# Two-layer backbone on one core: the next layer's norm woven into the layer end, gate blocks moved into the router, the attention's weight pairs reordered

## The reference

```python
shift1, scale1, gate1, shift2, scale2, gate2 = split(silu(c) @ w_mod[l] + b_mod[l], 6)
h = rms_norm(x, norm1_w) * (1 + scale1) + shift1
u_a, v_a, q, k, v, f_in, g = split(h @ w_in)         # 1024 -> 7680
y_a = chunk_gmlp(u_a, v_a, ...)                      # spatial gating, chunks of 128
y_b = diff_attention(rope(norm(q)), rope(norm(k)), v, lam)   # 8 heads, two maps each
y_c = fourier_mix(f_in)
merged = sum over b of sigmoid(g_b) * (y_b @ w_br_b)
x = x + gate1 * (merged @ w_out)
h2 = rms_norm(x, norm2_w) * (1 + scale2) + shift2
# router: 1 of 4 groups, then the top 2 of its 4 experts; 16 experts, D_EXPERT = 512
y = sum over e of gates[:, e] * ((silu(h2 @ w_g[e]) * (h2 @ w_u[e])) @ w_d[e])
x = x + gate2 * y
```

## Time and profile before

| what | value |
|---|---|
| three runs, us | 1627.60, 1633.40, 1635.53 (median 1633.4) |
| profiled execution, us | 1626.59, span 1624.7, granted clock 0.995 |
| PE busy | 1568.7 us, 97% of the span |
| VectorE busy | 1040.4 us, 64% |
| ScalarE busy | 926.4 us, 57% |
| POOL busy | 519.0 us, 32% |
| DMA | 381 MB, 234 GB/s over the span |
| chain that ended last | PE 74%, DMA 11%, VectorE 8%, ScalarE 3% |

### The profile page before, as it was taken

How to read it: one execution, slowest core, us unless ns; L and a number is a source line. 1 busy time by engine, 2 the same in 40 slices (tenths; PEclk the granted TensorE clock), 3 DMA queues, 4 the chain that set the end, 5 groups by cost and what they waited for, 6 DMA issues and landing times.

```text
span 1624.7 us, 21397 instructions
## 1 busy us (share of the span) xinstructions
PE 1568.7 (97%) x7755; PEld 1235.0 (76%) x7755; DVE 1040.4 (64%) x1366; ACT 926.4 (57%) x1298; POOL 519.0 (32%) x263
## 2 busy tenths in 40 slices
PE   7999999999999999999999999999999989999998
PEld 5677877876876787888777778777778768888886
DVE  2226566673354888999962356667633569999997
ACT  4434444444444888888844344544443558888884
POOL 2344554443530311111134446534435221111101
PEclk9999999999999999999999999999999999999999
DMA  9854342334348999999986543422343379999998
GB/s 361 277 202 166 124 131 83 103 122 155 105 168 287 357 383 366 358 370 371 366 253 208 196 165 104 142 91 91 131 145 117 97 270 377 380 381 361 373 381 259
DMA packets 153535, 380.98 MB, mean 234 GB/s; under 512 B 20963, under 2 KB 26789, under 8 KB 153436
## 3 DMA queue, kind: packets, MB, share of 16 engines
q1 hardware_dynamic: 122704, 325.32, 55.9%
q10 hardware_dynamic: 20140, 36.56, 6.4%
q0 software_dynamic: 10592, 17.78, 3.6%
HBM read 377.47 MB, written 27.93 MB: 250 GB/s over the span
## 4 chain that ended last, share of the span: by engine, by line
PE 74%; DMA 11%; DVE 8%; ACT 3%; issue 2%; SPq 0%; POOL 0%; ACTq 0%; DVEq 0%; POOLq 0%
PE ps L611 59%; PE ps L620 5%; DMA raw<-w_e_down 4%; DVE wxl L2521 4%; DMA raw<-w_e_up 3%; PE ps L644 2%; PE ps L961 2%; ACT wxh L1860 1%; DMA raw<-w_mod 1%; DMA y<-part_rows 1%; PE ps L891 1%; PE ps L989 1%; PE ps L1269 1%; PE ps L655 1%; PE ps L663 1%
## 5 line engine op out<-in xcount | busy, mean ns | idle before, releaser
L1999 POOL TENSOR_TENSOR wl<-raw,wh 128x1024 fp32r<-128x1024 f32 x168 | 413.4, 2465 | 521.0 <-ACT wh L1357 505.5
L2521 DVE TENSOR_TENSOR wxl<-raw,wxh 128x1024 fp32r<-128x1024 f32 x384 | 454.3, 1220 | 60.5 <-ACT wxh L1860 58.1
L1860 ACT ACTIVATE wxh<-raw 128x1024 fp32r<-128x1024 f32 x384 | 402.7, 1059 | 92.9 <-DMA raw<-w_e_gate 32.8
L611 PE MATMUL ps<-wxh,xeT 128*128 128x512 f32 x1024 | 342.1, 399 | 5.8 <-DVE xeT L2562 3.3
L1357 ACT ACTIVATE wh<-raw 128x1024 fp32r<-128x1024 f32 x168 | 176.7, 1055 | 220.2 <-PE ps L611 211.7
L611 PE MATMUL ps<-wh,hTh 128*128 128x512 f32 x720 | 294.4, 409 | 3.4 <-DVE hTl L2147 2.6
L611 PE MATMUL ps<-wh,hTl 128*128 128x512 f32 x720 | 282.7, 393 | 0.0
L611 PE MATMUL ps<-wl,hTh 128*128 128x512 f32 x720 | 282.0, 392 | 0.0
L611 PEld LDWEIGHTS ps<-wxh,xeT 128*128 128x128 f32 x1024 | 192.6, 188 | 51.1 <-DVE wxl L2521 5.0
L611 PE MATMUL ps<-wxl,xeT 128*128 128x512 f32 x512 | 199.5, 390 | 0.0
L611 PEld LDWEIGHTS ps<-wh,hTh 128*128 128x128 f32 x720 | 136.1, 189 | 38.7 <-issue 6.8
(11 more groups left out here) (295 smaller groups left out, 2164.4 us busy)
## 6 DMA issues: line engine op xcount, KB each, us to landing
raw<-w_e_gate SPq DMA_DIRECT2D x128, 512.0 KB, 6.8
raw<-w_e_up SPq DMA_DIRECT2D x128, 512.0 KB, 5.7
raw<-w_e_down SPq DMA_DIRECT2D x128, 512.0 KB, 5.6
raw<-w_in SPq DMA_DIRECT2D x120, 512.0 KB, 3.6
own<-w_mod ACTq DMA_DIRECT2D x27, 1024.0 KB, 7.6
raw<-w_mod SPq DMA_DIRECT2D x36, 512.0 KB, 6.0
raw<-w_br_b SPq DMA_DIRECT2D x16, 512.0 KB, 3.7
raw<-w_out SPq DMA_DIRECT2D x16, 512.0 KB, 3.6
```

The source lines that it names most:

```text
L611: ins = pe.matmul(out, act_hl[i], w_hl[j], start=start and n == 0, stop=stop and n == 2)
L1860: act.activation(wxh[:, q % RING_MOE, :, :], raw[:, place, :, :], ACT.Copy).then_inc(sem("hi_done"), 1)
L1999: pool.tensor_tensor(wl[:, p % RING, :, :], raw[:, PAIR_CHUNK[p] % RAW, :, :], wh[:, p % RING, :, :].bitcast(F32), ALU.subtract).then_inc( ...
L2521: dve.tensor_tensor(wxl[:, q % RING_MOE, :, :], raw[:, expert_chunk(l, 0, q)[0], :, :], wxh[:, q % RING_MOE, :, :].bitcast(F32), ALU.subtr ...
```

## The change

It has these parts; the diff names the same functions.

- Attention, both layers: one more pair is pumped ahead of the first head's transposes (`pump(5)`), one less behind them (`pump(1)`). Head 1 loses its extra pair between its scores and `turn_first`, and has one after `turn_second` as the other heads do.
- Layer end, layer 0 to 1. VectorE takes the mean of a tile as soon as its squares are there, and writes only the rows of tile 0 (`front_rows`), between units 3 and 4. For tiles 1 and 2 it computes the reciprocal root alone (`front_rms`) and counts `rms_ready`; ScalarE writes these rows (`front_rows` there). The root of a tile is taken right after its squares.
- ScalarE copies the first of the layer's weight pairs after the squares of tile 1, the second after the rows of tile 2, the third after the first pair of norm columns.
- SP waits for `y` of tile 0 alone before the loads of layer 1.
- Router of the last layer: half (10, 1) takes the place of the filler, half (11, 1) is moved from expert 0 to behind (11, 0).

```diff
--- before.py
+++ after.py
...
             if l:
-                for name in PARTS_IN:
-                    sp.wait_ge(sem(name), at(name, l - 1, PER[name]))
+                sp.wait_ge(sem(PARTS_IN[0]), at(PARTS_IN[0], l - 1, PER[PARTS_IN[0]]))
...
-            pump(4)
+            pump(5)
...
             turn_qk(0)
-            pump(2)
+            pump(1)
             scores(0)
...
                     scores(h + 1)
-                if h == 1:
-                    pump(1)
                 turn_first(h)
                 pump(1)
                 turn_second(h)
-                if h != 1:
-                    pump(1)
+                pump(1)
...
                 part(10, 0)
                 turn_tile(1)
-                spin(FILL_ROUTER[0], 5)
+                part(10, 1)
                 turn_tile(2)
...
                 back(1)
-                part(10, 1)
                 part(11, 0)
+                part(11, 1)
                 back(2)
...
                         token_sums(2, 2, ps[:, 0, 0:2])
-                        if not more:
-                            part(11, 1)
...
+            def front_rows(t):
+
+                act.wait_ge(sem("rms_ready"), t)
+                act.wait_ge(sem("xn_done"), at("xn_done", l, t))
+                act.activation(xn[:, t, :], x[:, t, :], ACT.Copy, scale=st[:, 9 + t:10 + t]).then_inc(sem("xn_done"), 1)
...
-                    if t:
-                        tile_root(t - 1)
-                    hi(DENSE0[l] + t)
-                tile_root(NT - 1)
+                    if t == 1:
+                        hi(DENSE0[l])
+                    if t == NT - 1:
+                        front_rows(1)
+                    tile_root(t)
+                front_rows(2)
+                hi(DENSE0[l] + 1)
...
                 norm_pair(0, R_NORM1, k)
+                if l and k == 0:
+                    hi(DENSE0[l] + 2)
...
+            def front_rms(l, t):
+
+                dve.wait_ge(sem("root"), at("root", l, t + 1))
+                return dve.reciprocal(st[:, 9 + t:10 + t], st[:, 6 + t:7 + t])
+
+            def front_rows(l, t):
+
+                link(front_rms(l, t))
+                dve.tensor_scalar(xn[:, t, :], x[:, t, :], st[:, 9 + t:10 + t], None, ALU.mult).then_inc(sem("xn_done"), 1)
...
-            tile_rows(0)
-            tile_rows(1)
-            tile_rows(2)
+            if l == 0:
+                tile_rows(0)
+                tile_rows(1)
+                tile_rows(2)
...
-            for u in range(NT, 2 * NT):
-                add_unit(u)
-                if l + 1 < DEPTH:
-                    front_mean(l + 1, u - NT)
+            if l + 1 < DEPTH:
+                front_mean(l + 1, 0)
+            add_unit(3)
+            if l + 1 < DEPTH:
+                front_rows(l + 1, 0)
+            add_unit(4)
+            if l + 1 < DEPTH:
+                front_mean(l + 1, 1)
+            add_unit(5)
+            if l + 1 < DEPTH:
+                front_rms(l + 1, 1).then_inc(sem("rms_ready"), 1)
+                front_mean(l + 1, 2)
+                front_rms(l + 1, 2).then_inc(sem("rms_ready"), 1)
```

More of the change, by code:

```diff
@@ L199 @@
     h2_copied=NT, h2_out=16 * (NT + 1), gate_ready=1,
-    pick_ready=PICKED, idx_acc=PICKED, idx_ready=PICKED, table=16 * (2 * NT + 2), pickT_ready=2, scattered0=16 * LOOSE // 2, scattered1=16 * LOOSE // 2, zeroed=16 * 6, parts_in2=16 * 2, parts_added=NT, X_acc=NE + 1, xe_hi=NE + 1, xe_ready=NE + 1,
+    pick_ready=PICKED, idx_acc=PICKED, idx_ready=PICKED, table=16 * (2 * NT + 2), pickT_ready=2, scattered0=16 * LOOSE // 2, scattered1=16 * LOOSE // 2, zeroed=16 * 6, parts_in2=16 * 2, rms_ready=DEPTH, X_acc=NE + 1, xe_hi=NE + 1, xe_ready=NE + 1,
     gathered0=16 * NE // 2 + 16, gathered1=16 * NE // 2 + 32, silu_done=NE,
```

## The result

| | before | changed kernel |
|---|---|---|
| median, us (runs) | 1629.82 (10) | 1619.05 (10) |
| lowest, highest | 1624.88, 1635.53 | 1615.35, 1626.07 |
| profiled execution, span | 1626.59, 1624.7 | 1615.35, 1613.6 |
| granted clock in it | 0.995 | 0.997 |

The ratio is 0.9934 with a 95% interval of 0.9914 to 0.9955: 7 to 14 us, the middle 10.8. The prediction said 1625.6 for the median and 7.75 us. The 57 further runs of the kernel before that were taken beside the experiments have a median of 1628.54, and against them the difference is 9.5 us.

The account below looks back on a forecast made before the run. TensorE, busy 97% of the span, was taken to bound the kernel; 2.8 (attention) + 1.15 (layer end) + 3.8 (gate blocks) = 7.75 us off the 1633.4 median gave 1625.6 us, range 1617.5 to 1632.5.

Parts of the forecast that it names:

- Attention: Both layers: head 1 goes from 14.60 to 13.18 us, 1.4 us gained a layer, 2.8 us in all.
- The moved pair: Ahead of the first head's transposes: pair and transposes change places, the gap of some 1.6 us stays; costed at nothing.
- The layer end, rows and filler: Layer 0 to 1: rows ready about 835.5, PE's filler last at 837.53, so the filler limits the gain.
- the 2.3 us: Layer end: first dense matmul at 840.3 instead of 842.60, before the price of the dead heat.
- The dead heat: Norm: POOL's third subtract beats VectorE's second split by some 0.05 us, PE loses about 1.15; rival R1, VectorE wins, 0.20.
- I take nothing: Layer 1's loads issued earlier: no gain or loss; reads of y have 2.2 us of cover before PE needs them.
- the rule of the round robin: DMA engines alternate between rings: last read of y lands near 825.5 to 827, sum up to 1.5 us smaller.
- gaining 1.15: Layer end: 2.3 us gained less 1.15 us lost to the dead heat; 2.3 kept as the other end.
- ScalarE's issues: Two issues of own<-w_mod ahead of ScalarE's first norm work, 4.21 us before: counted 0, lower end 0.4 us lost.
- The gate blocks: Last layer: half 2.0 and wait for pair 4 2.06 leave expert 0, router loses 0.25; net 3.8 us.
- The wait before expert 1: PE's wait for expert 1's gathered rows: stays at 2.05 us, as VectorE's queue moves with pair 4.
- R2: Rival, chance 0.15: the expert loop returns the head's gain because weights can't follow; all 3.8 us lost, 1629.4 us.

Follow-up runs that it names:

- b3: The changed kernel with SP again waiting for y of all three tiles before the loads of layer 1; one execution, 1619.15 us.
- b2: The changed kernel, filler cut from 30 to 22 rounds, weight copies two and three moved, POOL's third subtract after VectorE's second norm split; median 1614.83 us, ratio 0.992.
- b1: The changed kernel with ScalarE's third weight copy right behind the second instead of behind the first norm pair; ratio 0.9932.
- d1: Against b2: three of the six w_in loads wait for y of all tiles, the other three for tile 0 only; ratio 0.9931.
- a3: The kernel before with the gate-block edits alone, halves (10, 1) and (11, 1) moved in the router; median 1622.43 us, ratio 0.995.

## Why the prediction was right or wrong

**Attention.** Right in its size: 1.40 us a layer, and turn_first doesn't wait in head 1. The moved pair, costed at nothing, costs 0.13 to 0.15 us in layer 1 and about as much in layer 0: the wait is longer by 0.05, and the rest isn't placed. Net 2.5 instead of 2.8.

**The layer end, rows and filler.** Right: the rows were ready 4.3 us after the filler's start (829.49 - 825.15; 5.7 by the forecast's times), the filler was last, and b3 shows the 2.3 us. The row tile on VectorE took 0.75. The cut filler (b2) shows that the rows had room.

**The dead heat.** Right, POOL won by 0.15 us, and the price was 1.1 us as said; b1 takes it away. The Trainium skill (SBUF — State Buffer, "SBUF: two separate sides") names the reason: VectorE with two SBUF inputs and POOL hold a shared port exclusively for a whole instruction. The 2.63 against 0.55 us agrees.

**The loads: the step that failed.** "I take nothing" looked only at the reads of y. Those were covered: the longest took 9.2 us from issue to landing, 8.1 before, and PE didn't wait for it. The 2 to 4 us that the rule of the round robin was weighed with didn't come. Even the 1 us isn't shown to be the loads' doing: over all kernels the longest of the three reads took 8.9 to 10.0 us with six early loads, 8.1 to 8.9 with late ones, and up to 10.4 at the end of layer 1, with no next layer's loads beside it. Nor did the queues take turns at first. In the changed kernel the reads had the DMA engines to themselves from 812.2 to 815.2 us, though five loads were issued by then; its DMA view for that time has one queue:

```profile
q0 software_dynamic: 146, 0.53, 100.2%
```

The first packet of the loads came 2.6 to 4.2 us after their first issue in the eight kernels with early loads, and 1.0 us after it in the four with late ones.

The price came from a place that I hadn't looked at, PE's own pause at the flag, 1.29 us in the earlier trace rows, which I took as fixed. With early loads it is 1.98 to 4.17 us in all eight traces, with late loads 1.29 to 2.11 in four, and half clock followed in five of the eight and in none of the four. Why the pause is longer stays open. The layer end lost 0.5 us in the changed kernel's trace instead of gaining 1.15, which lies within the 0.8 us that unedited layer ends differ by; b3, without that edit, gains 1.11.

**ScalarE's issues.** Hidden, as said: 0.96 us where they took 4.21.

**The gate blocks.** The half and the wait for pair 4 went, 4.06 less the 0.32 that VectorE still costs. The wait before expert 1, which I left at 2.05, fell to 1.27, and the router lost 0.36 instead of 0.25. Net 4.2 instead of 3.8; R2 is wrong, the loop gives nothing back.

**The sum.** 2.5 - 0.5 + 4.2 = 6.2 us from the parts against 7.75. The timed 9.5 to 10.8 us contain something more. The mean granted clock of the timed runs is 0.9954 against 0.9939, which is 2.4 us at 1.71 for each 0.00106 (one stretch in some 1620 us). With it the parts come to 8.6, inside the interval of 7.3 to 14; the -0.5 already holds 0.9 us of half clock on the filler, so the two overlap by up to that. So the forecast was near for two reasons that partly cancel: a price that it missed, and a gain in clock that it didn't know of, and of which only a part has a place. That the size came out so near is partly luck. The median itself came 6.5 us under the 1625.6 of the forecast: 3.6 of these are the level, since the three runs that it started from had a median of 1633.4 and the ten have 1629.82. (The range's lower end is a slip of 0.2: 1626.6 less 8.9 is 1617.7.)

## What to carry to other kernels

Before a load is moved ahead, list every wait near it that DMA engines may have a part in, a pause at a branch among them, and not only the transfers that the diff names. A wait that the view calls "issue" isn't a constant; look at it in several traces. Where the work behind a filler is shortened, shorten the filler with it: here that, with the copies set apart, took 4.65 us off a layer end that the edits alone had left as it was, and 3.1 in d1, where half clock fell on the filler.

## What the runs showed of the hardware

A half-clock stretch had one size, some 3.4 us at 0.50 of the full clock with 1.71 us lost (one was twice that). Leaving out the one at the end of each trace, two to seven of them stood in each profiled execution. They stand behind places where PE had been idle, for 0.8 to 4.2 us, but not behind each of them, and filling the likeliest place moved them to the next in three cases of four. In the changed kernel's ten runs, from 1615 to 1626 us at clocks from 0.997 to 0.992, time and clock go closely together (correlation -0.89). Over the runs of all kernels, each taken against its own mean, they do so less (-0.66), and in a3's twelve runs not at all, so the clock is a part of the spread and not shown to be most of it.

TensorE's pause at a flag's read took 1.29 to 4.17 us and ended 1.42 to 1.46 us behind a packet of an instruction queue, while VectorE's at the same flag stayed at 1.52 to 1.54. Loads issued while POOL's accumulating reads were under way sent their first packet 2.6 to 4.2 us after the issue instead of 1.0.
